# An encoder layer in one core: products before the norm, and probabilities scaled on ScalarE

## What is computed

```python
h = x * (1.0 + scale[:, 0, None, :]) + shift[:, 0, None, :]
y = _swiglu(h, ffn1_w_in[l], ffn1_w_out[l])
x = _layernorm(ALPHA * x + 0.5 * gate[:, 0, None, :] * y, post_ln_g[l, 0], post_ln_b[l, 0])

h = x * (1.0 + scale[:, 1, None, :]) + shift[:, 1, None, :]
proj = h @ w_in[l]
cq, ckv, k_rope_raw, u = jnp.split(proj, split_at, axis=-1)
attn = _mla(cq, ckv, k_rope_raw, positions, q_norm_g[l], kv_norm_g[l], w_uq[l], w_ukv[l])
pooled = _multiscale_pool(u, pool_w[l], pool_b[l], pool_scale[l])
y = jnp.concatenate([attn, pooled], axis=-1) @ w_out[l]
x = _layernorm(ALPHA * x + gate[:, 1, None, :] * y, post_ln_g[l, 1], post_ln_b[l, 1])
...
```

## Time and profile before

| | |
|---|---|
| median of 3 runs | 1060.31 us (1060.1 to 1060.59) |
| profiled execution | 1060.47 us |
| its span | 1058.7 us |
| busy share PE / DVE / ACT / POOL | 91% / 50% / 32% / 22% |
| mean granted PE clock | 0.958 |

### The profile page before, as it was taken

The page is one execution under the profiler, slowest core; times in us unless marked ns, Lnnn a source line. Parts: engine busy times, 40 slices in busy tenths (PEclk is TensorE's granted clock), DMA queues, the critical chain, the costliest instruction groups (busy, mean ns, idle before and its releaser), DMA issues.

```text
span 1058.7 us, 10396 instructions
## 1 busy us (share of the span) xinstructions
PE 960.5 (91%) x4082; PEld 760.8 (72%) x4082; DVE 534.0 (50%) x681; ACT 343.1 (32%) x472; POOL 237.2 (22%) x183
## 2 busy tenths in 40 slices
PE   4999999999999996899899952899999999999992
PEld 3788888888878874677566640688888888878880
DVE  5956766445557538465587633832222222233225
ACT  4633232333212222464334314232333232212113
POOL 0021010100053103558200045541001010033110
PEclk7999999999999998999999986899999999999996
DMA  9745665655446430423111011043222222223202
GB/s 373 278 152 187 198 199 194 193 192 187 159 159 222 165 120 10 117 82 105 54 41 40 21 40 40 10 149 100 85 99 96 100 100 95 75 83 97 94 15 79
DMA packets 37985, 127.18 MB, mean 120 GB/s; under 512 B 4016, under 2 KB 4144, under 8 KB 37936
## 3 DMA queue, kind: packets, MB, share of 16 engines
q1 hardware_dynamic: 37936, 126.52, 35.6%
HBM read 123.36 MB, written 2.10 MB: 119 GB/s over the span
## 4 chain that ended last, share of the span: by engine, by line
PE 81%; DVE 9%; ACT 3%; POOL 3%; issue 2%; DMA 0%; SPq 0%; DVEq 0%; ACTq 0%; POOLq 0%
PE bank L490 24%; PE bank L492 24%; PE bank L491 24%; DVE ckv L1399 3%; PE bank L744 2%; PE bank L720 1%; PE bank L513 1%; PE bank L508 1%; POOL x L1450 1%; DVE x L1112 1%; DVE x L1118 1%; PE bank L509 1%; POOL s_sum L1458 1%; POOL q_sum L1460 1%; DVE act_t L1104 1%
## 5 line engine op out<-in xcount | busy, mean ns | idle before, releaser
L823 DVE TENSOR_TENSOR w_lo<-raw,w_hi 128x1024 fp32r<-128x1024 f32 x159 | 212.1, 1340 | 325.2 <-ACT w_hi L815 324.8
L490 PE MATMUL bank<-h_hi,w_hi 128*128 128x512 f32 x770 | 305.3, 397 | 8.1 <-DVE h_lo L1410 3.5
L492 PE MATMUL bank<-h_hi,w_lo 128*128 128x512 f32 x770 | 301.6, 392 | 0.0
L491 PE MATMUL bank<-h_lo,w_hi 128*128 128x512 f32 x770 | 301.5, 392 | 0.0
L815 ACT ACTIVATE w_hi<-raw 128x1024 fp32r<-128x1024 f32 x159 | 162.3, 1033 | 209.9 <-PE bank L492 209.7
L490 PEld LDWEIGHTS bank<-h_hi,w_hi 128*128 128x128 f32 x770 | 145.7, 189 | 40.3 <-DVE h_lo L1410 3.9
L491 PEld LDWEIGHTS bank<-h_lo,w_hi 128*128 128x128 f32 x770 | 145.9, 190 | 30.4 <-issue 0.7
L492 PEld LDWEIGHTS bank<-h_hi,w_lo 128*128 128x128 f32 x770 | 145.7, 189 | 30.6
L1442 POOL TENSOR_TENSOR a_lo<-act_t,a_hi 128x512 fp32r<-128x512 f32 x44 | 58.4, 1328 | 428.2 <-ACT a_hi L876 428.2
L490 PE MATMUL bank<-a_hi,w_hi 128*128 128x512 f32 x352 | 140.6, 399 | 0.0
L492 PE MATMUL bank<-a_hi,w_lo 128*128 128x512 f32 x352 | 139.0, 395 | 0.0
(11 more groups left out here) (212 smaller groups left out, 891.2 us busy)
## 6 DMA issues: line engine op xcount, KB each, us to landing
raw<-wunits SPq DMA_DIRECT2D x145, 512.0 KB, 3.3
ada_ring<-ada_w SPq DMA_DIRECT2D x56, 512.0 KB, 4.5
ada_first<-ada_w SPq DMA_DIRECT2D x16, 512.0 KB, 8.8
raw<-wunits SPq DMA_DIRECT2D x16, 384.0 KB, 2.9
x<-xT SPq DMA_DIRECT2D x4, 512.0 KB, 5.8
outT<-x SPq DMA_DIRECT2D x8, 256.0 KB, 2.0
K<-shift SPq DMA_DIRECT2D x2, 512.0 KB, 6.8
c_act<-c_rows SPq DMA_DIRECT2D x1, 512.0 KB, 7.7
```

What stands on the lines that cost most here:

```text
L490: mm(out, lh, rh, start=first, stop=False)
L491: mm(out, lh, rl, start=False, stop=False)
L492: return mm(out, ll, rh, start=False, stop=last)
L823: nc.vector.tensor_tensor(lo, raw[:, slot, 0:width], hi.bitcast(F32), SUB).then_inc(s_lo, 1)
```

## The change

It rebuilds four places.

Opening units. The first four units behind each of the first two norms run on x after the subtraction of the first tile's mean, times G = (1 + scale) g, with no root in it. The norm is put on the result: with r the reciprocal root and s = -mean r, a unit's output is r (W G x) + s (W G) + W B. The columns W G and W B come from 16 matmuls of 4 output rows over the four slots (`weight_sums`) and four of width 2 that turn them (`weight_columns`). DVE makes `r * bank` and adds `s * wg`; `wb` is a bias of the next operation. The statistics' matmuls stand inside the first opening unit. h of the other units is formed on ACT (`h_split`) instead of DVE, into `hn_hi` and `hn_lo` at the first norm. `first_units` goes.

Second norm. DVE subtracts the mean tile by tile (`mixer_shifted`), and POOL only adds.

Attention. ACT's exp also gives row sums (`accum_out`), DVE takes the reciprocal of a 128x1 column, and ACT scales the probabilities in place. V loses its ones. Transposes come three steps behind scores, values one step later. Fills fall from 14 to 10 (two parts in three steps); the last four output tiles run whole behind attention. Three pool groups move ahead of it.

SP. The gather of the rotary key into K waits for the end of the projection as well, and the layout of tiles in SBUF differs.

```diff
-FILL = ["q2", "q3", "q4", "q5", "p0", "p1", "p2", "p3", "q6", "q7", "p4", "p5", "p6", "p7"]
+FILL = ["q2", "q3", "q4", "q5", "p0", "p1", "q6", "q7", "p2", "p3"]
+FILL_STEP = [3 * i // 2 for i in range(2 * len(FILL))]
...
             sp.wait_ge(s_krp, 3)
+            sp.wait_ge(s_used, MX + N_PROJ)
...
-            def first_units(base, p):
-                for j in range(3):
-                    pe.wait_ge(s_lo, base + j + 1)
+            def whole_unit(n, out, p=0):
...
+            def weight_sums(p, base):
+                pe.wait_ge(s_lo, base + OPEN)
+                pe.wait_ge(s_gb, p)
+                out = bank[SUM_BANK[p]][0:4, :].rearrange("p (a b) -> p a b", b=P)
+                for i, part in enumerate((w_hi, w_lo)):
+                    for k in range(KD):
+                        last = mm(out, gb[:, p - 1, k, :], part[:, :, k * P:(k + 1) * P],
+                                  start=i == 0 and k == 0, stop=i == 1 and k == KD - 1)
+                last.then_inc(s_r, 1)
+            def weight_columns(p):
+                pe.wait_ge(s_rc, p)
+                for i in range(SLOTS):
+                    last = mm(bank[SUM_BANK[p]][:, 2 * i:2 * i + 2], s_sum[0:4, i * P:(i + 1) * P], sel[0:4, :],
+                              start=True, stop=True)
+                last.then_inc(s_sel, 1)
+            def opening(p, base):
+                if p == 2:
+                    pe.wait_ge(s_er, SPLIT_TILES)
+                for j in range(OPEN):
+                    pe.wait_ge(s_lo, base + j + 1)
+                    for k in range(KD):
+                        if j == 0:
+                            if k == 3:
+                                if p == 2:
+                                    stats_begin(p)
+                                stats_mean(p)
+                            elif k == 4:
+                                stats_square(p)
+                            elif k == KD - 1:
+                                weight_sums(p, base)
+                            pe.wait_ge(s_ul[p], k + 1)
+                        last = mm3(bank[OPEN_BANK[p][j]][:], w(base + j, k * P), open_h(p, k), k == 0, k == KD - 1)
+                    last.then_inc(s_used, 1)
+                    if j == 1:
+                        weight_columns(p)
...
+            opening(1, MX)
+            for t in range(OPEN, N_PROJ):
                 pe.wait_ge(s_lo, MX + t + 1)
-                if t >= 4:
-                    emptied(pe, t - 4)
-                whole_unit(MX + t, bank[t % 4][:])
-                if t == 4:
+                if t == 5:
+                    pe.wait_ge(s_wc, 1)
+                if t >= 6:
+                    emptied(pe, t - 6 if t < 10 else t - 4)
+                whole_unit(MX + t, bank[mix_bank(t)][:], 1)
...
+            pool_group(0)
+            pool_group(1)
...
-                pe.wait_ge(s_exp, k + 1)
+                pe.wait_ge(s_nrm, k + 1)
...
-                    pe.wait_ge(s_o, hd)
+                    pe.wait_ge(s_ml, hd)
...
+            attn_parts = {30: 0, 32: 1, 33: 2, 34: 3}
+            for step in range(STEPS + QB):
                 if step < STEPS:
                     scores(step)
-                if step < NPG:
-                    pool_group(step)
-                if 0 <= step - 2 < STEPS:
-                    transpose_probs(step - 2)
-                if step < 2 * len(FILL):
-                    fill(step // 2, step % 2)
...
+                if step == 2:
+                    pool_group(3)
+                if 0 <= step - 3 < STEPS:
+                    transpose_probs(step - 3)
+                if step in FILL_STEP:
+                    fill(*divmod(FILL_STEP.index(step), 2))
+                if step in attn_parts:
+                    attn_out(attn_parts[step], [0, 1])
+                if step >= 7 and step % QB == 3:
+                    values((step - 7) // QB)
+            for ks in ([2], [3]):
+                for m in range(SPLIT_TILES):
+                    attn_out(m, ks)
+            for m in range(SPLIT_TILES, KD):
+                out_tile(m)
 
             ffn(F2, 1, 2, a_hi2, a_lo2)
...
+                    act.wait_ge(s_nx[p], 2 * m + 2)
+                    if m >= 2:
+                        act.wait_ge(s_hl[p], m - 1)
+                    fn(act_t[:, m % 2, :], x[:, m, :], ACT.Identity, scale=G[:, p, m:m + 1],
+                       bias=B[:, p, m:m + 1]).then_inc(s_hf[p], 1)
                     act.wait_ge(s_hf[p], m + 1)
-                    fn(h_hi[:, m, :], act_t[:, m % 2, :], ACT.Copy).then_inc(s_hh[p], 1)
+                    fn(norm_h(p, m)[0], act_t[:, m % 2, :], ACT.Copy).then_inc(s_hh[p], 1)
+                    if m == 1:
+                        act.wait_ge(s_r, p)
+                        fn(s_sum[0:4, :], bank[SUM_BANK[p]][0:4, :], ACT.Copy).then_inc(s_rc, 1)
+                    if m == 2:
+                        act_hi(act, base + 1 + LEAD)
+                    if m == 5:
+                        act_hi(act, base + 2 + LEAD)
+            def plain_high(p, m):
+                if p == 1 and m == 0:
+                    act.wait_ge(s_xs[p], 1)
+                else:
+                    act.wait_ge(s_e[p], m + 1)
+                fn(open_h(p, m)[0], x[:, m, :], ACT.Identity, scale=G[:, p, m:m + 1]).then_inc(s_uh[p], 1)
...
+            opened(0, ckv[:, 0, 0:TOK], s_sum[:])
+            opened(1, ckv[:, 1, 0:TOK], sq[:, 0, :])
+            act_hi(act, MX + 3 + LEAD)
+            opened(3, cq[:, 0, :], q_sum[:])
...
-                       bias=nmax[:, step:step + 1]).then_inc(s_exp, 1)
-                if 0 <= step - 2 < STEPS:
-                    hd, i = divmod(step - 2, QB)
-                    act.wait_ge(s_t, step - 1)
+                       bias=nmax[:, step:step + 1], accum_out=rsum[:, step:step + 1]).then_inc(s_exp, 1)
+                if 1 <= step <= STEPS:
+                    n = ((step - 1) % QB + 1) * P
+                    p_block = prob[:, (step - 1) % 4, 0:n]
+                    act.wait_ge(s_inv, step)
+                    fn(p_block, p_block, ACT.Copy, scale=inverse[:, step - 1:step]).then_inc(s_nrm, 1)
+                if 0 <= step - 3 < STEPS:
+                    hd, i = divmod(step - 3, QB)
+                    act.wait_ge(s_t, step - 2)
...
+            def root(p, both_at, split=None):
 
                 dve.wait_ge(s_st[p], both_at)
                 dve.wait_ge(s_rq[p], 1)
                 stt(var[:], bank[SQR[p]][:], SUM_EPS, tmp[:], ADD, SUB).then_inc(s_rv[p], 1)
+                if split is not None:
+                    dve_lo(dve, split)
...
+            def plain_low(p, m):
+                dve.wait_ge(s_uh[p], m + 1)
+                hi, lo = open_h(p, m)
+                stt(lo, x[:, m, :], G[:, p, m:m + 1], hi.bitcast(F32), MUL, SUB).then_inc(s_ul[p], 1)
+            def weight_columns(p):
+                dve.wait_ge(s_sel, p)
+                cp(wcol[:], bank[SUM_BANK[p]][:, 0:2 * SLOTS]).then_inc(s_wc, 1)
+                dve.wait_ge(s_wc, p)
...
+            def opened(t, dst, rows=slice(0, P)):
+                dve.wait_ge(s_used, MX + t + 1)
+                tt(dst, bank[mix_bank(t)][rows, :], rstd[rows, :], MUL).then_inc(s_evd, 1)
+                dve.wait_ge(s_evd, t + 1)
+                stt(dst, shift[rows, :], wg(MX + t)[rows, :], dst, MUL, ADD).then_inc(s_un[1], 1)
...
+                if 1 <= step <= STEPS:
+                    dve.wait_ge(s_exp, step)
+                    nc.vector.reciprocal(inverse[:, step - 1:step], rsum[:, step - 1:step]).then_inc(s_inv, 1)
...
-                    nc.vector.reciprocal(inverse[r0:r0 + VDIM, :], bank[PV_BANK][z0:z0 + VDIM, :])\
-                        .then_inc(s_inv, 1)
-                    dve.wait_ge(s_inv, hd + 1)
-                    if hd >= 2:
-                        dve.wait_ge(s_ml, hd - 1)
-                    tt(attn[r0:r0 + VDIM, :], bank[PV_BANK][r0:r0 + VDIM, :], inverse[r0:r0 + VDIM, :], MUL)\
-                        .then_inc(s_o, 1)
...
+            def mixer_residual(m):
+                if m < SPLIT_TILES:
+                    dve.wait_ge(*((s_used, S_A + m // 2 + 1) if m % 2 else (s_ag, m // 2 + 1)))
+                else:
+                    dve.wait_ge(s_used, S_OUT + m - SPLIT_TILES + 1)
+                stt(x[:, m, :], y_bank(2, m)[:], gate[:, 1, m:m + 1], x[:, m, :], MUL, ADD).then_inc(s_er, 1)
+            def mixer_shifted(m):
+                dve.wait_ge(s_er, m + 1)
+                tt(x[:, m, :], x[:, m, :], shift[:], SUB).then_inc(s_e[2], 1)
+            for m in range(SPLIT_TILES):
+                mixer_residual(m)
+            lo_after(S_A + 1)
+            dve.wait_ge(s_cm[2], 1)
+            cp(shift[:], bank[MEAN[2]][:]).then_inc(s_cc[2], 1)
+            dve.wait_ge(s_cc[2], 1)
+            for m in range(SPLIT_TILES):
+                mixer_shifted(m)
+            for m in range(SPLIT_TILES):
+                plain_low(2, m)
+            for m in range(SPLIT_TILES, KD):
+                lo_after(S_OUT + m - SPLIT_TILES)
```

(26 more changed lines are left out.)

438 lines of the change are left out of this document (245 added, 193 removed).

## The result

| | before | after |
|---|---|---|
| median of 4 runs | 1060.2 us (1059.61 to 1060.59) | 1026.38 us (1026.16 to 1026.94) |
| ratio, 95% interval | | 0.968, [0.9665, 0.9699] |
| span of the profiled execution | 1058.7 us | 1024.7 us |
| PE busy | 960.5 us, 91% | 964.1 us, 94% |

The change makes the kernel 33.8 us faster. The forecast was 1003.8 with a range of 995 to 1022: the sign and the larger part are right, but the time lies above the range, 22.6 us over the forecast.

What follows compares the result with a forecast made beforehand. PE bounds the kernel, busy 960.5 of 1058.7 us; the gain is its idle and low-clock time. Terms -12.8 + 2.6 - 13.2 - 33.1 = -56.5 us gave 1003.8 against the median of 1060.31; forecast 995 to 1012, range 995 to 1022.

Steps and rivals of the forecast that it cites:

- PE's own work: Whole kernel: 40 more matmuls, nothing removed; weight sums 3.7 us, width-2 records 0.9, so the change pays by filling holes.
- Slack 6.5 us: the root is hidden.: First norm: last tile of hn at 26.7 us, PE needs it at 33.2; first norm and projection gain 12.8 us.
- a tile 1.31: First norm: VectorE's time to normalise one tile, counted as 8 x 1.3 us in the path to hn.
- GpSimd has 2.6 us of sums per tile: done as PE ends: Second norm: sums keep up with output tiles of 5.5 us each; opening 29.8 us, stage gain 33.1.
- Stage 686.7 to the end: unchanged.: From 686.7 us to the kernel's end: the stage keeps its 372.0 us.
- I cost it at nothing: Attention: 32 ScalarE scalings, 1.7 to 2.1 us a head, costed at nothing beside PE's steps; stage gain 13.2 us.
- the other 6.7 a head stay: Attention: scores, transposes, values and their gaps keep 6.7 us of each 12.2 us head cycle, 53.6 for 8 heads.
- Rival 1: Attention: ScalarE sets the pace through its exps' waits; +26 us if whole, half gives 1017; chance 0.12.
- Rival 2: Norm openings cover less as GpSimd and VectorE slow each other; PE waits before unit five, twice: +13, 1017; chance 0.07.
- Rival 3: Openings: plain parts or weight sums come late and PE waits for the root after all; about 1028; chance 0.04.
- Rival 4: Attention: longer chain through one in-order queue stalls PE once a head; +59 us, 1063, slower than before; chance 0.02.
- Signs named ahead: Norms, attention: no h_hi waits after roots, statistics within 6 us, ScalarE 60 to 70%; wrong if cq or w_lo waits exceed 3.

Runs made afterwards that it cites:

- e1: Changed kernel with GpSimd's low parts of both normalised tiles h on 8 of 512 columns, first norm's products using the high part instead: 1017.1 us.
- e10: Changed kernel with the first norm's queues in order of need (GpSimd's squares before scaling x; VectorE's fourth-unit eviction and two splits moved): 1019.5 us.
- e3: Changed kernel with VectorE doing the second norm's residual and shift of tiles 4 to 7 before low parts and splits: 1023.2 us.
- e9: Changed kernel with GpSimd's sums of the second norm on 8 of 512 columns from the second addition on: 1017.9 us.
- e11: Changed kernel with VectorE's second-norm queue in order of need: residual and shift first, fewer low parts and splits between: 1019.1 us.
- e13: Changed kernel with both norms' queues in order of need and three more weight splits moved: 1008.0 us.
- e5: Changed kernel with the 32 scalings of the probabilities moved from ScalarE to VectorE, each behind its reciprocal: 1021.2 us.
- e6: Changed kernel with the 32 scalings of the probabilities moved from ScalarE to GpSimd: 1018.5 us.
- e7: Changed kernel with ScalarE's scalings of the probabilities run on 8 of up to 512 columns: 1022.2 us.

## Why the prediction was wrong, point by point

- **PE's own work:** right. The 16 weight sums took 3.7 us (402.75 to 406.44, as forecast), the eight width-2 records 1.05 (0.9), the opening 28.4 (28.4).
- **"Slack 6.5 us: the root is hidden."** Right for the root, wrong in its size. The term "a tile 1.31" was read where GpSimd was idle; the loop took 20.1 us, not 13.1. The last tile of hn came at PE's last moment (a wait of 0.4). I followed this chain to hn only; the work queued behind the loop on VectorE, and GpSimd's scaling of x ahead of `s_sum`, had no slack. That is where most of the 6.9 us went: the stage takes 72.8 us in e1 and 73.1 in e10 (78.6 in the changed kernel).
- **The second norm, "GpSimd has 2.6 us of sums per tile: done as PE ends".** This step failed most, 9.0 us. A pair of sums takes 3.3 beside VectorE (1.57 and 1.74 above), and VectorE's low parts and splits, which the step did not count at all, grow from 0.74 and 1.2 to 1.7 and 2.3. The residual of tile 4 starts at 607.83, when PE is about to end tile 6, and the later ones keep that distance (e3, e9, e11).
- **"Stage 686.7 to the end: unchanged."** 4.6 us too low. A wait of 1.8 us for the split of the seventh up unit stands right after the opening, and in the changed kernel seven starts 0.43 us apart follow a microsecond later. e1 removes the wait, since the loop in front ends earlier, and so does e13 by order; the stage then takes 367.1 and 367.4 us, under 1 us above the forecast. With the wait but without the slow starts it takes 369.5 (e5, e6).
- **"I cost it at nothing", the scalings.** Wrong: 5.5 to 8.2 us (e5, e6). The stage's sum, 117.6 against 119.4, looked right by luck, because the other terms were off the other way: with the scalings on GpSimd the stage takes 111.1, so the terms that were priced were 6.5 us too much in all. Which of them was not taken apart; "the other 6.7 a head stay" is the largest that was carried over unchanged. A sum that fits does not prove its terms.
- **Keys, values and queries:** right, 20.6 against 20.2.
- **Rival 1** had the right mechanism with too large a price, 13 us for 8. **Rival 2** had the right mechanism, "GpSimd and VectorE slow each other", and gave it 0.07. It let PE wait before unit five; PE waited at the sums and splits instead. Both came at once, which the forecast did not allow for: its range went to either, not to their sum. **Rival 3**'s 1028 lies near the measured 1026.4 by accident: no wait for the root stayed. **Rival 4** did not happen.
- **Signs named ahead:** no wait for h_hi after the roots, ScalarE busy 63% in attention: as said. Waits for `cq` and `w_lo` of 5.2 and 3.4 us, and statistics 8.2 us behind the last output tile (614.8 to 623.0) and not 6: the signs of a wrong forecast, as named there.

## What to carry to other kernels

Before a chain's length is taken from a trace, look at what GpSimd does in that row: if it will work beside VectorE in the new kernel, look for a row of the old one where both worked, and take that duration. When work is hidden behind PE, follow each helper's queue past the result that PE wants first, to everything queued behind it, for the next wait shows up there. And a spare engine share says little about a step's chain: e7 and e6 gained 4 and 8 us from an engine that was idle a third of the time.
